# Meta keys' part of the second layer's values as one 96-row product of high and low halves, in place of a full fp32 product

## The reference, cut to what matters

```python
N_META = 16
Q_BLOCK = 128

def _mla_attention(q_nope, q_pe, k_nope, k_pe, v):
    ...
        s = (jnp.einsum('bhqd,bhkd->bhqk', qn, k_nope) + jnp.einsum('bhqd,bkd->bhqk', qp, k_pe)) * scale
        s = jnp.where(rel >= 0, s, -jnp.inf)
        p = jax.nn.softmax(s, axis=-1)
        return jnp.einsum('bhqk,bhkd->bhqd', p, v)

def _diff_attention(q, k, v, lam, slopes):
    ...
        p = jax.nn.softmax(s, axis=-1)
        w = p[:, :, 0] - lam * p[:, :, 1]
        return jnp.einsum('bhqk,bhkd->bhqd', w, v)

    h = jnp.concatenate([meta, x], axis=1)
    ...
    y = _rmsnorm(h, final_norm_w)
    return y[:, N_META:N_META + S]
```

## Time and profile before

| | |
|---|---|
| Median of 3 runs | 1639.9 us (1638.22 to 1641.71) |
| The profiled execution, its own time | 1644.14 us |
| Its span from first to last instruction | 1642.3 us |
| PE, PE's weight loads, DVE, ACT, POOL busy | 1620.0, 1344.9, 845.1, 819.8, 675.8 us |
| Attention of the second layer (four passes) | from 1040 to 1375 us |
| Meta keys' value products (L1123) | 64 products, 128 pairs of weight load and matmul |

### The profile page before, as it was taken

How to read it: one execution, slowest core, us unless ns; L and a number is a source line. 1 busy time by engine, 2 the same in 40 slices (tenths; PEclk the granted TensorE clock), 3 DMA queues, 4 the chain that set the end, 5 groups by cost and what they waited for, 6 DMA issues and landing times.

```text
span 1642.3 us, 22656 instructions
## 1 busy us (share of the span) xinstructions
PE 1620.0 (99%) x8343; PEld 1344.9 (82%) x8343; DVE 845.1 (51%) x1934; ACT 819.8 (50%) x1759; POOL 675.8 (41%) x569
## 2 busy tenths in 40 slices
PE   9999999999999999999999999999999999999998
PEld 7788898888888887888888887888877777878886
DVE  3346656564213756467545451432245455767674
ACT  3346666765333454454445456444456565344561
POOL 4453434334666700667110124644444335655022
PEclk9999999999999999999999999999999999999999
DMA  6454546455778877857998947745554414624762
GB/s 220 131 154 99 159 91 183 94 148 111 175 176 197 231 224 226 269 154 203 243 258 252 241 140 264 230 129 141 152 162 102 132 53 144 141 100 129 244 243 103
DMA packets 139595, 281.13 MB, mean 171 GB/s; under 512 B 11051, under 2 KB 19052, under 8 KB 139324
## 3 DMA queue, kind: packets, MB, share of 16 engines
q1 hardware_dynamic: 86012, 160.29, 29.9%
q0 software_dynamic: 31664, 81.70, 24.2%
q10 hardware_dynamic: 21808, 37.68, 7.2%
HBM read 254.68 MB, written 92.06 MB: 211 GB/s over the span
## 4 chain that ended last, share of the span: by engine, by line
PE 90%; DVE 4%; ACT 2%; issue 2%; POOL 1%; DMA 1%; POOLq 0%; ACTq 0%; DVEq 0%
PE acc L686 17%; PE acc L688 17%; PE acc L687 17%; PE turn L783 3%; PE acc L827 2%; PE acc L826 2%; PE acc L828 2%; PE turn L1122 2%; PE turn L828 2%; PE turn L827 2%; PE turn L826 2%; PE sc L828 2%; PE sc L827 2%; PE sc L826 2%; PE turn L708 2%
## 5 line engine op out<-in xcount | busy, mean ns | idle before, releaser
L1808 POOL TENSOR_TENSOR w_lo<-w_raw,w_hi 128x512 fp32r<-128x512 f32 x341 | 507.6, 1497 | 723.9 <-ACT w_hi L1238 723.0
L1238 ACT ACTIVATE w_hi<-w_raw 128x512 fp32r<-128x512 f32 x565 | 353.2, 628 | 432.1 <-PE acc L688 233.0
L686 PE MATMUL acc<-w_hi,setA_hi 128*128 128x512 f32 (+1 forms) x1088 | 443.9, 408 | 6.5 <-DVE setA_lo L2007 3.1
L688 PE MATMUL acc<-w_hi,setA_lo 128*128 128x512 f32 (+1 forms) x1088 | 421.5, 387 | 0.0
L687 PE MATMUL acc<-w_lo,setA_hi 128*128 128x512 f32 (+1 forms) x1088 | 420.2, 386 | 0.0
L686 PEld LDWEIGHTS acc<-w_hi,setA_hi 128*128 128x128 f32 x1088 | 205.2, 189 | 44.8 <-issue 6.1
L688 PEld LDWEIGHTS acc<-w_hi,setA_lo 128*128 128x128 f32 x1088 | 204.5, 188 | 42.6
L687 PEld LDWEIGHTS acc<-w_lo,setA_hi 128*128 128x128 f32 x1088 | 205.7, 189 | 29.7
L2199 DVE TENSOR_TENSOR w_lo<-w_raw,w_hi 128x512 fp32r<-128x512 f32 x224 | 155.5, 700 | 143.5 <-ACT w_hi L1238 143.2
L1323 ACT ACTIVATE p_w<-sm,negm 128x256 f32<-128x256 f32 (+1 forms) x128 | 60.6, 474 | 56.5 <-DVE sink_d L2076 56.5
L1645 ACT ACTIVATE p<-sm,negm 128x144 f32<-128x144 f32 (+3 forms) x96 | 54.3, 565 | 52.3 <-DVE negm L2510 34.4
(11 more groups left out here) (519 smaller groups left out, 3108.2 us busy)
## 6 DMA issues: line engine op xcount, KB each, us to landing
w_raw<-in_swa_w_in SPq DMA_DIRECT2D x35, 1024.0 KB, 7.5
w_raw<-in_w_in SPq DMA_DIRECT2D x32, 1024.0 KB, 5.6
w_raw<-sum_out SPq DMA_DIRECT2D x64, 256.0 KB, 4.3
sum_k<-in_w_in POOLq DMA_DIRECT2D x24, 512.0 KB, 7.0
sum_out<-in_swa_w_out POOLq DMA_DIRECT2D x24, 512.0 KB, 7.7
sum_v<-in_w_in POOLq DMA_DIRECT2D x24, 512.0 KB, 9.0
w_raw<-in_w_in SPq DMA_DIRECT2D x48, 256.0 KB, 5.4
sum_out<-in_w_out POOLq DMA_DIRECT2D x24, 512.0 KB, 6.6
```

The lines of the kernel that those rows point to most:

```text
L686: mm(acc[t][:, 0:cols], hi[:, kc, rows], wh, start=(k == 0), stop=False)
L688: last = mm(acc[t][:, 0:cols], lo[:, kc, rows], wh, start=False, stop=(k == K - 1))
L1238: nc.scalar.activation(w_at(f)[0], raw_of(f), ACT.Copy).then_inc(done, 1)
L1808: nc.gpsimd.tensor_tensor(lo, raw_of(f), hi.bitcast(F32), ALU.subtract).then_inc(s_lo, 1)
```

## The change

Each of the 16 meta columns of p and 16 meta rows of v is split into an fp32r high half and the rest. They are laid out so that one product of 96 rows adds three: p columns 0 to 15 hold the high half, 32 to 47 the high half again, 64 to 79 the low half; v rows 0 to 15 the high half, 32 to 47 the low half, 64 to 79 the high half; the rows between are zeros. So high-high, high-low and low-high come from one fp32r matmul. For this

- DVE gets `split_p_meta` in every `combine` (two instructions a unit; in MLA ahead of the reciprocal, in DIFF behind the sum, for which it waits), and `split_v_meta` once a head, at step 12 + 12 head + 3 behind everything else of that step (two copies and a subtraction of 16 rows);
- PE turns `p_meta`, 96 columns, as the last instead of the first of a unit, behind a new wait for `p_split`, and waits for `v_split` before the first values of a head;
- ACT's second copy in `keep_pT2` takes 96 rows instead of 16;
- the zeros are set in other tiles (three memsets for two before MLA, one more before DIFF).

```diff
--- before.py
+++ after.py
@@ -206,7 +206,9 @@
         diff_km = over("diff_km", [META, HEADS * VD], MASK + 4 * KEYS)
         km_hi = over("km_hi", [P, HEADS * META], B_HI + 32128, F32R)
         natm_k = over("natm_k", [META, 2, VD], MISC + 12672)
-        natm_v = over("natm_v", [P, 2, VD], MISC + 13696)
+        natm_v = over("natm_v", [META, 2, VD], MISC + 13696)
+        vm_mla0, vm_diff0 = over("vm_mla0", [P, VD], MISC + 14720, F32R), over("vm_diff0", [P, VD], MISC + 13184, F32R)
+        vm_1 = over("vm_1", [P, VD], MISC + 16832, F32R)
         stage_m = over("stage_m", [META, CW], MISC)
         stage_m0 = over("stage_m0", [META, 320], STAGE)
         cqT_hi = over("cqT_hi", [P, 4, S], B_HI, F32R)
@@ -232,7 +234,8 @@
         alibi = over("alibi", [P, ALIBI_AT[NT]], B_HI + 26752)
         kpeT_lo = over("kpeT_lo", [P, KEYS], B_HI + 29952, F32R)
         pT2 = over("pT2", [P, 2, S], WORK)
-        pTm = over("pTm", [P, 2, P], WORK + 4096)
+        pTm = over("pTm", [P, 2, P], WORK + 4096, F32R)
+        p_meta = over("p_meta", [P, 2, FULL], WORK + 7232, F32R)
         rope_t = over("rope_t", [P, 4, NT, ROPE // 2], WORK + 5120)
         metaT = sb("metaT", [P, META_UNITS, META], F32R)
         alibi_h = over("alibi_h", [P, 2, ALIBI_AT[NT]], MASK)
@@ -373,6 +376,8 @@
                 self.full, self.free, self.score, self.m, self.p, self.pv, self.o = (
                     sem(f"s_{kind}_{n}") for n in ("full", "free", "score", "m", "p", "pv", "o"))
                 self.rope = sem("s_mla_rope") if self.mla else None
+                self.p_split, self.v_split = sem(f"s_{kind}_p_split"), sem(f"s_{kind}_v_split")
+                self.vm = (vm_mla0 if self.mla else vm_diff0, vm_1)
                 self.w, self.slope = (None, None) if self.mla else (sem("s_diff_w"), sem("s_diff_slope"))
 
         MLA, DIFF = Attend("mla"), Attend("diff")
@@ -1105,10 +1110,10 @@
                 if not A.mla and j == NT - 2:
                     pe.wait_ge(s_far, 2 * (4 * i + u // NT + 1))
                 src = p2[:, u % 2, 0, KEYS - width(j):]
-                nc.tensor.transpose(turn[1][0:META, P:2 * P], src[:, 0:META], ident[:])
                 for b in range(j + 1):
-                    last = nc.tensor.transpose(turn[0][:, b * P:(b + 1) * P], src[:, META + b * P:META + (b + 1) * P], ident[:])
-                last.then_inc(A.full, 1)
+                    nc.tensor.transpose(turn[0][:, b * P:(b + 1) * P], src[:, META + b * P:META + (b + 1) * P], ident[:])
+                pe.wait_ge(A.p_split, i * NU + (u + 1))
+                nc.tensor.transpose(turn[1][0:FULL, P:2 * P], p_meta[:, u % 2].bitcast(F32), ident[:]).then_inc(A.full, 1)
 
             def values2(A, i, u):
                 head, j = u // NT, u % NT
@@ -1117,10 +1122,11 @@
                 pe.wait_ge(A.free, i * (4 * A.batches + NU) + ((count["t0"] if A.mla else turned_at[u]) + 1))
                 if j == 0:
                     pe.wait_ge(A.ld_v[buf], (i * 2 + (head // 2 + 1)) * 32)
+                    pe.wait_ge(A.v_split, i * 4 + head + 1)
                 dst = turn[1][:, 2 * P:3 * P]
                 for b in range(j + 1):
                     mm(dst, pT2[:, u % 2, b * P:(b + 1) * P], nat_v[:, buf, b], start=(b == 0), stop=False)
-                mm(dst, pTm[:, u % 2], natm_v[:, buf], start=False, stop=True).then_inc(A.pv, 1)
+                mm(dst, pTm[0:FULL, u % 2], A.vm[buf][0:FULL], start=False, stop=True).then_inc(A.pv, 1)
                 count["pv"] += 1
 
             def attend_body(A, i, c0):
@@ -1651,7 +1657,7 @@
                 count["t0"] += 1
                 act.wait_ge(A.pv, i * NU + (u + 1))
                 nc.scalar.activation(pT2[:, u % 2, 0:n], turn[0][:, 0:n], ACT.Copy)
-                nc.scalar.activation(pTm[0:META, u % 2], turn[1][0:META, P:2 * P], ACT.Copy).then_inc(A.free, 1)
+                nc.scalar.activation(pTm[0:FULL, u % 2], turn[1][0:FULL, P:2 * P], ACT.Copy).then_inc(A.free, 1)
 
             count = {"t0": 0}
 
@@ -1924,7 +1930,7 @@
                 kd, at_ = (kvb_d, (4 * i + head) * 2 * VD + VD) if A.mla else (kv_d, (HEADS + 4 * i + head) * VD)
                 cols = slice(at_, at_ + VD)
                 pool.dma_start(nat_v[:, buf], by_rows(kd, cols)).then_inc(A.ld_v[buf], 16)
-                pool.dma_start(natm_v[0:META, buf], kd[S:KEYS, cols]).then_inc(A.ld_v[buf], 16)
+                pool.dma_start(natm_v[:, buf], kd[S:KEYS, cols]).then_inc(A.ld_v[buf], 16)
 
             def before(A, i, head):
 
@@ -2479,8 +2485,9 @@
 
             dve.wait_ge(s_used, B[26] + 4)
             dve.wait_ge(s_short[0], 4 * 16)
-            V.memset(natm_v[:], 0.0)
-            after(dve, V.memset(pTm[:], 0.0))
+            for vm in MLA.vm:
+                V.memset(vm[:].bitcast(F32), 0.0)
+            after(dve, V.memset(p_meta[:].bitcast(F32), 0.0))
             V.memset(tick[:], 0.0).then_inc(s_zero, 1)
 
             def soften2(A, i, u, comp):
@@ -2514,12 +2521,32 @@
 
                 b, lo = u % 2, S - (u % NT + 1) * P
                 dve.wait_ge(A.p, i * NU * A.comps + (u + 1) * A.comps)
+                if A.mla:
+                    split_p_meta(A, b, lo)
                 after(dve, V.reciprocal(rden_2[:, b, 0:A.comps], den_2[:, b, 0:A.comps]))
                 if not A.mla:
                     after(dve, V.scalar_tensor_tensor(coef[:, b:b + 1], den_2[:, b, 0:1], neglam[:, 0:1], rden_2[:, b, 1:2],
                                                       ALU.mult, ALU.mult))
                     V.scalar_tensor_tensor(p2[:, b, 0, lo:], p2[:, b, 1, lo:], coef[:, b:b + 1], p2[:, b, 0, lo:],
                                            ALU.mult, ALU.add).then_inc(A.w, 1)
+                    dve.wait_ge(A.w, i * NU + u + 1)
+                    split_p_meta(A, b, lo)
+
+            def split_p_meta(A, b, lo):
+
+                src = p2[:, b, 0, lo:lo + META]
+                twice = p_meta[:, b, 0:64].rearrange("p (r c) -> p r c", c=32)[:, :, 0:META]
+                after(dve, V.tensor_copy(twice, src.unsqueeze(1).to_broadcast([P, 2, META])))
+                V.tensor_tensor(p_meta[:, b, 64:64 + META], src, p_meta[:, b, 0:META].bitcast(F32), ALU.subtract).then_inc(A.p_split, 1)
+
+            def split_v_meta(A, i, head):
+
+                buf = head % 2
+                vm, src = A.vm[buf], natm_v[:, buf]
+                dve.wait_ge(A.ld_v[buf], (i * 2 + (head // 2 + 1)) * 32)
+                V.tensor_copy(vm[64:64 + META], src)
+                after(dve, V.tensor_copy(vm[0:META], src))
+                V.tensor_tensor(vm[32:32 + META], src, vm[0:META].bitcast(F32), ALU.subtract).then_inc(A.v_split, 1)
 
             def keep_o2(A, i, u):
                 head, j = u // NT, u % NT
@@ -2544,6 +2571,7 @@
                 dve.wait_ge(s_km, 1)
                 after(dve, V.tensor_tensor(km_lo[:], turn[1][:, 0:HEADS * META], km_hi[:].bitcast(F32), ALU.subtract))
                 V.memset(tick[:, 0:1], 0.0).then_inc(s_km, 1)
+                V.memset(vm_diff0[:].bitcast(F32), 0.0)
                 for half in range(2):
                     last = V.memset(km_in_q[:, half, :, VD:QB].bitcast(F32), 0.0)
                 after(dve, last)
@@ -2583,8 +2611,10 @@
                         for b in range(A.batches):
                             if not A.mla and Q == turn_time(A, head, b):
                                 low_head(i, head, b)
-
-            for A, body in ((MLA, 4 + NU), (DIFF, 2 * NU)):
+                        if Q == unit_time(NT * head) + 3:
+                            split_v_meta(A, i, head)
+
+            for A, body in ((MLA, 8 + 2 * NU), (DIFF, 4 + 3 * NU)):
                 if not A.mla:
                     meta_blocks()
                 first = link.n
```

## The result

The changed kernel takes **1664.2 us** in the median of 4 runs (1660.3 to 1669.2), the kernel before 1640.8: ratio 1.0147 (95% interval 1.0123 to 1.0170), 23.4 us slower. Forecast were 1656.2, 16.3 us slower. So the measured time lies in the stated range, 1642 to 1665, by 0.8 us, and above the forecast's own band of 1649 to 1663. The profiled execution took 1663.53 us, its span is 1661.6.

The account below looks back on a forecast made before the run. PE was taken to bound the kernel, in DIFF through a closed chain DVE, ACT, PE. DIFF +17.4 and MLA -1.1 gave +16.3 us on 1639.9, so 1656.2; range 1642 to 1665, forecast's own band 1649 to 1663.

Parts of the forecast that it names:

- rival 4: MLA's v split loses to POOL's subtraction, PE waits 1.2 us longer in each of 8 heads: +9, 1665; chance 0.07.
- One slot of 0.11 us per product: PE's meta product takes one load slot instead of two: 64 x 0.11 = 7.0 us saved, 3.5 each in MLA and DIFF.
- What DIFF keeps of it: Of DIFF's 3.5 us saved most is lost at waits; about one product in four keeps its 0.11: 0.9 us.
- Block 3, 1.26 us, the middle of two bounds: DIFF: `keep_o2` later behind POOL's subtraction, 1.15 us if only the split's subtraction is held, 1.37 if the cast is too.
- Block 1, v's split, 4.9 us in DIFF and 1.3 in MLA: DIFF: copies wait for POOL, delaying block 2's chain, 4.9 us; MLA: a head's first values wait 0.16 x 8 = 1.3 us.
- MLA, -1.1 us: MLA's sum: 3.5 us saved, less 1.3 for v's split and 1.1 for block 3's held cast.
- behind DVE's stand `soften2` and the rotation, for which I count nothing: MLA: both a step or more ahead of their readers, so 0; without that cover up to 0.42 us a unit.
- I had 1.1: MLA block 3: PE waits for p's split behind a held cast, at most 1.7 us, at least 0.5; 1.1 taken.
- signs I had named: Included PE idling 0.5 us or more ahead of DIFF block 2's values; wrong if MLA isn't shorter.
- Rival 1: The saving comes through and DIFF's waits don't: -5.7 us, 1634.2; chance 0.11.
- Rival 2: DVE costs only its own time, POOL never holds it: DIFF +7.6, MLA -2.2, total +5.4, 1645.3; chance 0.15.
- Rival 3: The fp32r product of 128 columns takes two slots, nothing saved: +4.4 on the forecast, 1660.6; chance 0.05.

Follow-up runs that it names:

- mla_placed_2: Against the kernel before: change in MLA alone, p's split ahead of `keep_o2`, v's split a unit early except in the very first head; 1637.6 us, ratio 0.9982.
- v_early_2: Changed kernel with `split_v_meta` hung on the head before's last unit, except MLA's very first head (step 15); 1654.6 us, ratio 1.0086 to the kernel before.
- diff_memsets: Changed kernel, but in DIFF two memsets replace p_meta's cast and subtraction and the meta keys' part is left out; 1651.5 us, ratio 1.0069 to the kernel before.
- clock_filled: Changed kernel plus 9 unread 512-column products on PE before the last unit's turns of each DIFF pass; 1660.8 us, ratio 1.0130 to the kernel before.
- mla_only_128: Against the kernel before: change in MLA alone, DIFF's fp32 product keeping 128 rows with 112 zeros; 1642.9 us, ratio 1.0013.
- mla_only: Against the kernel before: change in MLA alone, DIFF given an fp32 meta product of 16 rows and no split; 1648.8 us, ratio 1.0048.

## Why the prediction was right or wrong

The direction was right, and for DIFF the places and the mechanism. For MLA the sign was wrong, and the clock wasn't in the sum at all; the sum was 7 us short. That the time still lay in the range was luck: its upper end, 1665, came from rival 4, which wasn't what happened. Point by point:

- *One slot of 0.11 us per product*: right, 0.09 to 0.17 us a unit (mla_placed_2, v_early_2).
- *What DIFF keeps of it*: right in effect. v_early_2, without falls and without v's wait, shows a head as -0.16 and -0.12 (products of blocks 0 and 1), +0.70 (block 2's chain), -0.11, +1.52 (block 3's turn), -0.15 us. The +0.70 are the 0.42 of the split and the 0.28 that blocks 0 and 1 had gained. Eight heads cost 13.9 where the terms gave 12.5.
- *Block 3, 1.26 us, the middle of two bounds*: mis-sized. The cast was held in all 8 heads, so the upper bound, 1.37, was true: 0.9 us more. The rule of the Trainium skill, *VectorE: DVE Perf Modes*, section "What auto-detection actually checks", spoke for it, and this trace agrees (1.14 us for 0.18). In diff_memsets memsets at the same place aren't held, 0.14 us beside L1814. That fits the exclusive lock in the Trainium skill, *SBUF — State Buffer*, section "SBUF: two separate sides", which names DVE's two-input and 2-port operations.
- *Block 1, v's split, 4.9 us in DIFF and 1.3 in MLA*: right; 4.8 (18.7 less 13.9) and 1.4 to 1.5. It was a cost of the place alone.
- *MLA, -1.1 us*: wrong, +1.0. The step that failed is "behind DVE's stand `soften2` and the rotation, for which I count nothing". In block 2 the cast was held too, and all behind it moved. The changed kernel in MLA, head 1:

```profile
1070.10 0.35 DVE L2555 TENSOR_SCALAR o_nat<-turn,rden 128x128 f32<-128x128 f32 x1 [2.63 <-PE turn L1129]
1070.37 0.79 DVE L2539 CAST p_meta<-p 128x32 fp32r<-128x32 f32 x1
...
1072.94 0.70 DVE L2517 CUSTOM_DVE_ANT_0 sm<-sc,mask 128x528 f32<-128x528 f32 x1
...
1075.13 1.27 POOL L1814 TENSOR_TENSOR w_lo<-w_raw,w_hi 128x512 fp32r<-128x512 f32 x1 [3.47 <-ACT w_hi L1244]
1075.27 1.16 DVE L2540 TENSOR_TENSOR p_meta<-p,p_meta 128x16 fp32r<-128x16 f32 x1
...
1076.49 0.12 PEld L1116 LDWEIGHTS turn<-ident,p_meta 128*96 128x96 f32 x1 [0.34 <-DVE p_meta L2540]
```

  The `soften2` at 1072.94 is block 3's. It starts 2.84 us behind `keep_o2`, before it was 2.22 (1075.21 to 1077.43). ACT makes w's high half behind that exponential, and L1814 waits for it: it starts 5.03 us behind the same `keep_o2`, not 4.67, and so ends deeper in PE's turning. Block 3 cost about 3 us in MLA: PE's load of `p_meta` waited for L2540 once in each of the 8 heads, 3.0 us together. The experiments agree: v_early_2 and mla_placed_2 differ by 2.1, and the latter gives away some 0.8 in its first unit and in block 1 of five heads. I had 1.1 (and "1.7 us at most" should have been 1.5, 6 x 0.09 and 2 x 0.5). That block 2's held cast is what moves L1814 is read from the timelines; mla_placed_2 took away the holds of both blocks at once, and no run parts them.
- *The clock*: missing. Two falls, 3.1 us, the difference in DIFF between this trace and clock_filled's. I had counted PE's idle time and never asked what follows it.
- *Outside attention* the trace differs by -5.0 us before it and +1.5 after it (a third fall, at 1466). These aren't the change's.

In sum: 16.3 + 0.9 (cast) + 2.1 (MLA) + 3.1 (clock) = 22.4, of 22.8 us between MLA's start and DIFF's end. With -5.0 before and +1.5 after, the traces differ by 19.3 us, less than the medians' 23.4, since the trace before is of a slower execution. Of the signs I had named, two failed. MLA isn't shorter, which I had written down as a sign of being wrong. And PE doesn't idle longer ahead of block 2's values (0.51 us, 0.48), but ahead of its turn, 1.03 us. The chain reached PE one instruction earlier than I had read it.

Rival 1 falls with the 1.74 us above. Rival 2 describes diff_memsets, whose DIFF lost 9.3 us where it had 7.6; the changed kernel isn't that one. Rival 3 falls with the loads above. Rival 4 was real in mla_only_128, in one of its 8 heads, and in no other kernel.

## What to carry to other kernels

Price an added DVE operation by the moment at which it starts: 0.18 us, or the rest of POOL's operation. And then look for the moment: the change loses 23 us in the whole kernel as it was placed, and gains 2.5 in MLA alone where it is placed well. When a step on DVE gets longer, follow what it releases over ACT to POOL, for that is how a collision moves into a place that was free. Where a change makes PE stand idle for about 2 us, add what the clock may cost.

## What was not expected of the hardware

- **The clock falls after short idle times, but not always.** Over the traces of all 13 kernels PE stood idle for 1.95 to 2.14 us 22 times. 11 times the clock went to 0.50 for 3.4 us, from 0.2 us before PE began again to 1.3 us after. It never did behind the 1.3 us gaps of block 3. With idle times of 6.5 to 6.8 us it stood at 0.50 for 6.8 us, 3 times of 3, and fell while PE was still idle. One gap of 2.14 us stands in the kernel before too (at 1446), where it had no fall, while other kernels fell there. Two longer gaps, of 2.27 and 2.47 us, had none. The scatter of the kernel before goes with it: of 23 runs the 10 with a mean granted clock of 0.999 took 1638.3 to 1640.2 us, the 9 with 0.998 1639.0 to 1643.6, the 4 with 0.997 or less 1643.1 to 1645.4. By itself 0.002 of the clock is 3.3 us, so other waits take a part too.
- **An fp32 product of 16 rows among ones of 128 costs 0.2 to 0.39 us more** than with 112 rows of zeros (mla_only against mla_only_128), where no idle time behind it takes this up. Behind the change's fp32r product of 96 rows the next load follows after 0.12 us.
- **A cast of 32 columns is held by POOL like an operation with two inputs**, 1.14 us instead of 0.18, and so is a cast of v's 16 rows, 1.38 us instead of 0.22.
